# Order of VectorE's and ScalarE's work inside the sevens of a down projection

## What is computed

```python
def conv_ffn(h, w_up, conv_w, w_down):
    up = h @ w_up
    ...
    gate, val = conv[..., :D_FF], conv[..., D_FF:]
    return (jax.nn.gelu(gate, approximate=True) * val) @ w_down    # (256, 8192) @ (8192, 2048)
```

## Time and profile before

| | us |
|---|---|
| median of three runs | 1572.65 (1572.12 to 1572.96) |
| the profiled execution | 1572.21 |
| its span, first to last instruction | 1570.4 |
| PE busy (matmul) / weight loads | 1561.6 (99%) / 1354.2 (86%) |
| DVE busy | 1309.9 (83%) |
| ACT busy | 860.0 (55%) |
| DMA, mean over the span | 233 GB/s |

### The profile page before, as it was taken

How to read it: one execution, slowest core, us unless ns; L and a number is a source line. 1 busy time by engine, 2 the same in 40 slices (tenths; PEclk the granted TensorE clock), 3 DMA queues, 4 the chain that set the end, 5 groups by cost and what they waited for, 6 DMA issues and landing times.

```text
span 1570.4 us, 24827 instructions
## 1 busy us (share of the span) xinstructions
PE 1561.6 (99%) x8686; PEld 1354.2 (86%) x8686; DVE 1309.9 (83%) x1838; ACT 860.0 (55%) x1150; POOL 2.3 (0%) x14
## 2 busy tenths in 40 slices
PE   9999999999999999999999999999999999999998
PEld 8888888888888888888888888888888888888886
DVE  6566767687797798888888888888888999979997
ACT  6544644556565654444554445444444566666764
POOL 0000000000000000000000000000000000000000
PEclk9999999999999999999999999999999999999999
DMA  9896554556566567777677767777677689868884
GB/s 367 277 231 196 174 175 163 187 161 213 192 242 218 154 199 243 227 228 225 217 241 226 232 215 222 237 226 234 210 232 232 246 305 321 312 249 324 315 312 156
DMA packets 247622, 366.42 MB, mean 233 GB/s; under 512 B 6769, under 2 KB 211217, under 8 KB 246673
## 3 DMA queue, kind: packets, MB, share of 16 engines
q1 hardware_dynamic: 243872, 360.70, 69.4%
q10 hardware_dynamic: 3696, 5.00, 1.4%
HBM read 339.20 MB, written 26.48 MB: 233 GB/s over the span
## 4 chain that ended last, share of the span: by engine, by line
PE 99%; DVE 0%; ACT 0%; issue 0%; DVEq 0%
PE ps L1707 44%; PE ps L1711 23%; PE ps L1800 15%; PE ps L2015 10%; PE ps L1850 3%; PE ps L1813 1%; PE ps L1722 1%; PE ps L1727 0%; PE ps L1872 0%; PE ps L1938 0%; PE ps L1924 0%; PE ps L1958 0%; PE ps L1964 0%; PE ps L2085 0%; DVE arena L1683 0%; PE ps L1751 0%
## 5 line engine op out<-in xcount | busy, mean ns | idle before, releaser
L1707 PE MATMUL ps<-actT,w_hi 128*128 128x512 f32 x3072 | 715.0, 389 | 0.0
L539 ACT ACTIVATE w_hi<-raw 128x1024 fp32r<-128x1024 f32 x420 | 432.1, 1054 | 475.3 <-PE ps L1711 232.9
L1707 PEld LDWEIGHTS ps<-actT,w_hi 128*128 128x128 f32 x3072 | 569.3, 188 | 112.3 <-issue 0.2
L994 DVE TENSOR_TENSOR w_lo<-raw,w_hi 128x1024 fp32r<-128x1024 f32 x422 | 506.4, 1222 | 159.4 <-ACT w_hi L539 156.4
L1711 PEld LDWEIGHTS ps<-actT,w_lo 128*128 128x128 f32 x3072 | 372.1, 188 | 9.2 <-issue 0.7
L1711 PE MATMUL ps<-actT,w_lo 128*128 128x256 f32 x3072 | 377.3, 279 | 0.0
L1800 PE MATMUL ps<-w_hi,xs 128*128 128x512 f32 x672 | 184.1, 389 | 0.1
L1800 PEld LDWEIGHTS ps<-w_hi,xs 128*128 128x128 f32 x672 | 126.0, 188 | 26.5 <-issue 0.5
L2015 PE MATMUL ps<-actT,s_parts 128*128 128x512 f32 x480 | 125.0, 390 | 0.0
L1561 DVE SCALAR_TENSOR_TENSOR arena<-arena,convw 128x256 f32<-128x256 f32 x256 | 106.7, 479 | 0.0
L2015 PEld LDWEIGHTS ps<-actT,s_parts 128*128 128x128 f32 x480 | 89.3, 188 | 20.1 <-DVE actT L1336 1.9
(11 more groups left out here) (196 smaller groups left out, 1014.0 us busy)
## 6 DMA issues: line engine op xcount, KB each, us to landing
raw<-in_w_up_dram SPq DMA_DIRECT2D x128, 1024.0 KB, 6.1
raw<-in_w_down_dram SPq DMA_DIRECT2D x64, 1024.0 KB, 6.6
raw<-in_w_in_dram SPq DMA_DIRECT2D x58, 1024.0 KB, 5.2
token_forms<-xs SPq DMA_DIRECT2D x30, 768.0 KB, 7.7
s_parts<-token_forms SPq DMA_DIRECT2D x32, 704.0 KB, 5.5
raw<-in_w_o_dram SPq DMA_DIRECT2D x16, 1024.0 KB, 5.3
raw<-in_w_a_out_dram SPq DMA_DIRECT2D x8, 1024.0 KB, 5.3
raw<-in_w_b_out_dram SPq DMA_DIRECT2D x8, 1024.0 KB, 5.3
```

What stands on the lines that cost most here:

```text
L539: act.activation(w_hi[:, h % RING, :], raw[:, h // 2, h % 2 * HALF:(h % 2 + 1) * HALF], ACT.Copy)\
L994: dve.tensor_tensor(lo, raw[:, h // 2, h % 2 * HALF:(h % 2 + 1) * HALF], w_hi[:, h % RING, :].bitcast(F32), ALU.subtract).then_inc(lo_read ...
L1707: return pe.matmul(ps[:, bank + c, :], w_hi[:, h % RING, at:at + P], actT[:, k, :, :].rearrange("p a s -> p (a s)"), start=start, stop=stop)
```

## The change

On DVE, inside `down_middle`:
- `sum_blocks` falls apart into `block_differences`, `second_difference` and `last_difference`. The differences of a seven's blocks move up into the unit in front: between the two halves if that is a stored unit, between the rests of first and second sums if it is a seven.
- The rest of b22 stands ahead of the pair's rest, between second and last difference. PE's first products therefore wait for the second of these rests (`unit.lo + 2`).
- For the second seven of a pair (`unit.second`), the rest of half 0 of the stored unit behind it moves up, between the rests of the first and of the second sums (`half_behind_second`); the stored unit itself (`behind_second`) then has only half 1 left.

On ACT, the rounding of that half 0 moves up too: behind the tokens of the second seven and ahead of its pair (`between`).

No operation is added or left out. The diff:

```diff
--- before.py
+++ after.py
@@ -363,6 +363,8 @@
             def __init__(self, sweep, u):
                 super().__init__(sweep, u)
                 self.stored = sweep.stored <= u < STORED
+                self.second = self.seven and u - 1 in sweep.sevens and u + 1 in sweep.middle and u + 1 not in sweep.sevens
+                self.behind_second = not self.seven and u in sweep.middle and u - 1 in sweep.sevens and u - 2 in sweep.sevens
                 n = self.forms - FORMS[1]
                 self.summed, self.hi, self.lo = WO_SUMS + DOWN_SUMS * n, WO_HALVES + DOWN_HI * n, WO_HALVES + DOWN_LO * n
                 self.turn, self.part, self.part_landed = n, n % 2, 16 * (n // 2 + 1)
@@ -802,13 +804,15 @@
                 act.wait_ge(raw_landed[unit.slot], unit.landed)
                 act.activation(w_hi[:, slot, :], raw[:, unit.slot, j * HALF:(j + 1) * HALF], ACT.Copy).then_inc(hi_ready, 1)
 
-            def round_given_blocks(unit):
+            def round_given_blocks(unit, between=None):
 
                 block = raw[:, unit.slot, :]
                 act.wait_ge(raw_landed[unit.slot], unit.landed)
                 act.wait_ge(half_used, unit.part_free)
                 act.activation(b22_parts[unit.part][0], block[:, 3 * BLK:4 * BLK], ACT.Copy).then_inc(form_hi, 1)
                 act.activation(a_parts[:, unit.part, :], given(unit), ACT.Copy).then_inc(form_hi, 1)
+                if between:
+                    between()
                 if unit.turn:
                     act.wait_ge(first_products_done, unit.turn)
                 act.activation(two(pair_hi), quarters(block)[:, :, 0, :], ACT.Copy).then_inc(form_hi, 1)
@@ -832,12 +836,14 @@
                         round_given(unit)
                         round_sums(unit)
                     elif unit.seven:
-                        round_given_blocks(unit)
+                        after = DownUnit(sweep, u + 1)
+                        round_given_blocks(unit, between=(lambda: b_half(after, 0)) if unit.second else None)
                         round_block_sums(unit)
                         if unit.first and behind_first:
                             behind_first()
                     else:
-                        b_half(unit, 0)
+                        if sweep is wo_sweep or not unit.behind_second:
+                            b_half(unit, 0)
                         b_half(unit, 1)
 
             def copy_p1(sweep):
@@ -1358,40 +1364,93 @@
                 rest(b_lo[:, BT + 2 * BLK:BT + 4 * BLK], sweep.sums[:, 1, :], b_hi[:, BT + 2 * BLK:BT + 4 * BLK])\
                     .then_inc(lo_ready, 2)
 
-            def rest_of_given_blocks(unit):
+            def stored_half(unit, j):
+
+                slot = (unit.place + j) % RING
+                dve.wait_ge(hi_ready, unit.before + j + 1)
+                rest(w_lo[:, slot, :], raw[:, unit.slot, j * HALF:(j + 1) * HALF], w_hi[:, slot, :]).then_inc(lo_ready, 1)
+
+            def stored_unit(unit):
+
+                for j in range(2):
+                    stored_half(unit, j)
+
+            def half_behind_second(unit, seven):
+
+                slot = unit.place % RING
+                dve.wait_ge(hi_ready, seven.before + 1)
+                rest(w_lo[:, slot, :], raw[:, unit.slot, 0:HALF], w_hi[:, slot, :]).then_inc(lo_ready, 1)
+
+            def block_differences(unit, previous):
 
                 block = raw[:, unit.slot, :]
+                dve.wait_ge(form_lo, previous.lo + 3)
+                dve.wait_ge(raw_landed[unit.slot], unit.landed)
+                dve.tensor_tensor(two(unit.sweep.block_sums[:, 0, :]), quarters(block)[:, :, 1, :], quarters(block)[:, 0, :, :],
+                                  ALU.subtract).then_inc(form_summed, 1)
+
+            def second_difference(unit, previous):
+
+                sums = unit.sweep.block_sums
+                dve.wait_ge(form_summed, unit.summed + 1)
+                dve.wait_ge(lo_ready, previous.before + 2 + previous.second)
+                dve.tensor_tensor(sums[:, 1, 0:BLK], raw[:, unit.slot, 3 * BLK:4 * BLK], sums[:, 0, 0:BLK], ALU.subtract)\
+                   .then_inc(form_summed, 1)
+
+            def rest_of_second_block(unit):
+
+                dve.wait_ge(form_hi, unit.hi + 1)
+                rest(b22_parts[unit.part][1], raw[:, unit.slot, 3 * BLK:4 * BLK], b22_parts[unit.part][0]).then_inc(form_lo, 1)
+
+            def last_difference(unit):
+
+                sums = unit.sweep.block_sums
+                dve.wait_ge(form_summed, unit.summed + 2)
+                dve.tensor_tensor(sums[:, 1, BLK:2 * BLK], raw[:, unit.slot, 2 * BLK:3 * BLK], sums[:, 1, 0:BLK], ALU.subtract)\
+                   .then_inc(form_summed, 1)
+
+            def rest_of_pair(unit):
+
                 dve.wait_ge(form_hi, unit.hi + 3)
-                rest(two(pair_lo), quarters(block)[:, :, 0, :], two(pair_hi)).then_inc(form_lo, 1)
-                rest(b22_parts[unit.part][1], block[:, 3 * BLK:4 * BLK], b22_parts[unit.part][0]).then_inc(form_lo, 1)
-
-            def rest_of_block_sums(unit):
-
-                sums = unit.sweep.block_sums
+                rest(two(pair_lo), quarters(raw[:, unit.slot, :])[:, :, 0, :], two(pair_hi)).then_inc(form_lo, 1)
+
+            def rest_of_first_sums(unit):
+
                 dve.wait_ge(form_hi, unit.hi + 4)
-                rest(b_lo[:, BT:BT + 2 * BLK], sums[:, 0, :], b_hi[:, BT:BT + 2 * BLK]).then_inc(form_lo, 1)
+                rest(b_lo[:, BT:BT + 2 * BLK], unit.sweep.block_sums[:, 0, :], b_hi[:, BT:BT + 2 * BLK]).then_inc(form_lo, 1)
+
+            def rest_of_second_sums(unit):
+
                 dve.wait_ge(hi_ready, unit.before + 2)
-                rest(b_lo[:, BT + 2 * BLK:BT + 4 * BLK], sums[:, 1, :], b_hi[:, BT + 2 * BLK:BT + 4 * BLK])\
+                rest(b_lo[:, BT + 2 * BLK:BT + 4 * BLK], unit.sweep.block_sums[:, 1, :], b_hi[:, BT + 2 * BLK:BT + 4 * BLK])\
                     .then_inc(lo_ready, 2)
 
-            def stored_unit(unit):
-
-                for j in range(2):
-                    slot = (unit.place + j) % RING
-                    dve.wait_ge(hi_ready, unit.before + j + 1)
-                    rest(w_lo[:, slot, :], raw[:, unit.slot, j * HALF:(j + 1) * HALF], w_hi[:, slot, :]).then_inc(lo_ready, 1)
-
             def down_middle(sweep):
 
+                previous = None
                 for u in sweep.middle:
-                    unit = DownUnit(sweep, u)
-                    if not unit.seven:
-                        stored_unit(unit)
+                    unit, after = DownUnit(sweep, u), DownUnit(sweep, u + 1)
+                    if unit.seven:
+                        if unit.first:
+                            rest_of_second_block(unit)
+                        else:
+                            second_difference(unit, previous)
+                            rest_of_second_block(unit)
+                            last_difference(unit)
+                        rest_of_pair(unit)
+                        rest_of_first_sums(unit)
+                        if after.seven:
+                            block_differences(after, unit)
+                        if unit.second:
+                            half_behind_second(after, unit)
+                        rest_of_second_sums(unit)
+                        previous = unit
                     else:
-                        if not unit.first:
-                            sum_blocks(unit, unit.before)
-                        rest_of_given_blocks(unit)
-                        rest_of_block_sums(unit)
+                        if not unit.behind_second:
+                            stored_half(unit, 0)
+                        if after.seven:
+                            block_differences(after, previous)
+                        stored_half(unit, 1)
 
             def b_half(unit, j):
 
@@ -2027,7 +2086,7 @@
                 if down:
                     pe.wait_ge(form_hi, unit.hi + 3)
                     pe.wait_ge(s_parts_landed[unit.part], unit.part_landed)
-                pe.wait_ge(form_lo, unit.lo + 1 if down else HALVES_HI * unit.forms + 3)
+                pe.wait_ge(form_lo, unit.lo + 2 if down else HALVES_HI * unit.forms + 3)
                 firsts = together((p1, p2))
                 if down:
                     firsts.then_inc(first_products_done, 1)
```

More of the change, by code:

```diff
@@ L1359, in rest_of_sums @@
                     .then_inc(lo_ready, 2)
-            def rest_of_given_blocks(unit):
-                block = raw[:, unit.slot, :]
-                dve.wait_ge(form_hi, unit.hi + 3)
-                rest(two(pair_lo), quarters(block)[:, :, 0, :], two(pair_hi)).then_inc(form_lo, 1)
-                rest(b22_parts[unit.part][1], block[:, 3 * BLK:4 * BLK], b22_parts[unit.part][0]).then_inc(form_lo, 1)
-            def rest_of_block_sums(unit):
-                sums = unit.sweep.block_sums
-                dve.wait_ge(form_hi, unit.hi + 4)
```

(22 more changed lines are left out.)

## The result

The changed kernel takes 1574.55 us (median of 21 runs, 1573.65 to 1575.11), the kernel before in the same comparison 1572.17 us (21 runs, 1571.48 to 1572.96): 2.4 us more, a ratio of 1.0014 with a 95% interval of 1.0008 to 1.0020 (1.3 to 3.1 us). Forecast were 1574.8 us and +2.1 us. The profiled execution took 1574.01 us with a span of 1572.2.

What follows compares the result with a forecast made beforehand. PE was taken to bound the kernel, 99% busy. Ten pairs at 0.22 us less 0.12 gave +2.1 us: 1574.3 on the profiled execution, 1574.8 us with the median 0.44 above it; range 1572.3 to 1576.2.

Steps and rivals of the forecast that it cites:

- What bounds: Down projection: PE is busy 99% of the span; DVE, busy 24.65 of 25.21 us, is mostly hidden.
- The 0.62 us: Loss of the ten pairs to DVE, 9 x 0.05 + 0.17 us; all this stretch can give back.
- The lead of 0.18 to 0.19 us: How much earlier than a matmul is due DVE must finish its rest so that PE loses nothing.
- The sum for the pairs: Ten pairs at 0.22 us each, less 0.12 us once in the second sweep: +2.1 us.
- The half between the sums: Stored half on DVE between first and second sums: PE stands 0.21 to 0.22 us per pair, 2.2 us in all.
- 0.82 us as free: Room between first and second sums on DVE: 0.23 us waiting for ACT plus 0.59 us to spare; the half takes 1.13.
- The first pair of the second sweep, -0.12 us: First sums there can begin some 0.12 us sooner, taking that pair's loss back to 0.05 us, once.
- ACT's early half: Rounding half of the stored unit early on ACT fits with 1.7 us to spare and costs 0.
- rival 3: ACT's early half waits for its block's load beyond 9.1 us, holding PE: 1576.5 to 1579 us; chance 0.07.
- the 9.1 us forecast: Landing time of the stored unit's block load that would be free before ACT's pair round is held up.
- Rival 2: DVE hands over slower, half and second sums 1.25 us apart: 0.46 us a pair, 1577.1 us; chance 0.09.
- DVE's times: DVE's busy time stays; its waits in a rhythm grow by about 0.7 us.

Runs made afterwards that it cites:

- the half behind the second sums: Changed kernel with one line moved: DVE makes the stored half's rest after the second sums' rest of a pair's second seven; 1572.16 us, ratio 1.0000.
- the cuts: Changed kernel with the stored half's rest split around the second sums, 512, 768 or 896 columns in front: 1572.14 us (11 runs), 1573.12 and 1572.42 us (once each).
- the cut at 896: Changed kernel with 896 columns of the stored half's rest between first and second sums and 128 behind the second; 1572.42 us, run once.
- both halves: Changed kernel with both halves of the stored unit made between first and second sums on DVE and both rounded early on ACT; 1586.04 us, ratio 1.0085.

## Why the prediction was right, point by point

- **What bounds.** Right: singles stayed at 4.76 us and stored units at 5.44 to 5.46 in every version, apart from the start of the second sweep, and no version came under the time of before by more than its interval. The 0.62 us that DVE cost PE was the ceiling, and the half behind the second sums, with the full relief of DVE, got 0.20 of it by its pairs (0.12 in the first of the second sweep).
- **The lead of 0.18 to 0.19 us.** Right. It was read off the seventh matmul and used for the sixteenth: 0.22 us forecast in a pair, 9.79 - 9.57 = 0.22 measured, and the cuts place the beginning of the loss where that lead puts it, to within 0.02 us.
- **The time itself.** The sum for the pairs holds: +2.1 forecast, +2.11 in the chain. That 1574.8 came so near to 1574.55 is in part luck. Its base, 1572.65, was the median of three runs, and twenty-one gave 1572.17; the whole difference by the runs is 2.4, and 0.3 of that is in no term of the sum, though within the interval.
- **The half between the sums.** Right in place, price and number. It costs alone (1574.58 without the rest of the change), and the rest of the change costs nothing that the runs show without it (1572.16). The sentence that gave 0.82 us as free was off by 0.08; the sum did not use it.
- **The first pair of the second sweep, -0.12 us.** Right: 9.89 with the half alone, 9.80 with the whole change, and 9.57 for 9.69 with the half behind. Its cause is a little more mixed than told: the weight load of the first products now waits there as well (0.17 us with the half behind).
- **ACT's early half and rival 3.** The cover was real and was used. In the pair of units 10 and 11 the block of unit 12 took 8.5 us to land. More was free than the 9.1 us forecast: the prediction kept the load's issue where it was, 8.75 us ahead of the pair (1277.16 against 1285.91), but the relieved DVE releases the slot earlier, and the load goes out 9.84 us ahead (1275.76 against 1285.60). Free were 1286.99 - 1.05 - 1275.76 = 10.2 us. The issue, then ACT's wait for the block, and the pair's round behind it still waiting for PE:

```profile
1275.76 0.37 SPq L492 DMA_DIRECT2D raw<-in_w_down_dram  x1
...
1284.30 1.06 ACT L805 ACTIVATE w_hi<-raw 128x1024 fp32r<-128x1024 f32 x1 [0.97 <-DMA raw<-in_w_down_dram]
1286.99 1.06 ACT L818 ACTIVATE actT<-raw 128x1024 fp32r<-128x1024 f32 x1 [1.63 <-PE ps L2074]
```

- **Rival 2 and the Trainium skill's rule on the pipe.** The half and the second sums began 1.14 us apart and not 1.25, and each begins 0.08 us before the one in front has ended; with 1.25 the pairs would have taken 10.0 us. The Trainium skill, "VectorE: DVE Perf Modes", section "The DRAIN you can't avoid", says that the next operation does not start until the pipe is empty, but the same paragraph adds that a next operation that is not held starts earlier. The prediction gave the first of these without the second; the rows here agree with the second. Where they differ from the section is in its sentence that the semaphore costs nothing extra: an operation that waits for DVE's own last result begins 1.25 us after it (1286.16 to 1287.41), one that does not 1.14.
- **DVE's times.** Here a sign was wrong: its busy time was to stay, and it fell by 6.9 us, its idle time in a rhythm grew by 0.9 and not 0.7. The operations are the same and as long as before, but fewer of them wait for DVE's own last result, so more of them overlap with the one in front, and busy time counts an overlap once: behind the first difference of blocks the next operation began 1.25 us later before (1286.16 to 1287.41) and begins 1.14 later now (1293.60 to 1294.74). It did not touch the sum.

## What to carry to other kernels

Where an engine is nearly always busy, the busy share does not say what an operation costs there; the gates do. For each place where it could go, take the time until the next gate that the bounding engine waits for, subtract what must still be done before it and the lead that the waiting engine needs, and put the operation where it fits; if it fits nowhere, cut it. Read that lead off a place in the old trace where the engine did wait, and count free time from starts, not from the idle times of the rows.

## What the runs showed of the hardware

- PE loses less than its weight loads wait. A load that waited 0.17 us cost 0.05 us, one that waited 0.22 (the cut at 896) cost 0.09, 0.35 cost 0.22, and 1.50 (both halves) cost 1.35: 0.12 to 0.15 us less each time, however long the wait. The load after a late one follows after 0.11 us in place of 0.227 (1293.73 and 1293.84), so that part of the wait is caught up.
- The start of the second sweep, which the change does not touch, is the part of this stretch that scatters most. PE waits there for DVE's rest of an early half, which stands behind sums that wait for a block's load; by the starts of its matmuls against their rhythm of 0.2267 us it lost between 0.13 and 0.91 us there in the nine profiled executions (0.35 before, 0.51 after, 0.91 with the half behind the second sums). The two kernels in the old order lost 0.28 and 0.35 there, six of the seven in the new order 0.5 to 0.9, and the seventh 0.13. One profile for each version does not tell whether the new order has a share in it. That is left open; it is a scatter of the size of the 0.6 us that could have been gained.
